# A blocked triangular inverse inside an RWKV-7 layer: joining two passes of small products, and splitting one level into 32x32 blocks

## What is computed

```python
sa = jnp.einsum('bhvk,bhk->bhv', S, kk_t)
S = (S * w_t[:, :, None, :]
     - sa[..., None] * (kk_t * a_t)[:, :, None, :]
     + v_t[..., None] * k_t[:, :, None, :])
y = jnp.einsum('bhvk,bhk->bhv', S, r_t)
```

## Time and profile before

| what | value |
| --- | --- |
| median of 3 runs | 2400.12 us (2399.1 to 2400.26) |
| span of the profiled execution, first to last instruction | 2399.3 us |
| its mean granted PE clock | 0.998 |
| PE busy | 2361.7 us, 98% |
| DVE busy | 1534.4 us, 64% |
| ACT busy | 1209.0 us, 50% |

### The profile page before, as it was taken

How to read it: one execution, slowest core, us unless ns; L and a number is a source line. 1 busy time by engine, 2 the same in 40 slices (tenths; PEclk the granted TensorE clock), 3 DMA queues, 4 the chain that set the end, 5 groups by cost and what they waited for, 6 DMA issues and landing times.

```text
span 2399.3 us, 49369 instructions
## 1 busy us (share of the span) xinstructions
PE 2361.7 (98%) x20503; PEld 2229.2 (93%) x20503; DVE 1534.4 (64%) x1893; ACT 1209.0 (50%) x1590; POOL 17.1 (1%) x36
## 2 busy tenths in 40 slices
PE   9999999989999999999999999999999999999998
PEld 9999799879998899999999999999999888999886
DVE  8588588566774455657799875656745444555445
ACT  5586563354464466755644346465544333444343
POOL 0000000000000000000000000000000000000000
PEclk9999999999999999999999999999999999999999
DMA  9355566325556644564566565655666666666664
GB/s 285 116 184 175 178 191 187 99 74 179 180 169 187 189 151 158 180 201 141 158 193 179 165 184 167 185 179 150 199 199 173 191 190 186 185 184 183 193 186 148
DMA packets 216554, 419.90 MB, mean 175 GB/s; under 512 B 17056, under 2 KB 19440, under 8 KB 215648
## 3 DMA queue, kind: packets, MB, share of 16 engines
q1 hardware_dynamic: 207520, 397.98, 54.5%
q0 software_dynamic: 2560, 10.59, 1.4%
q10 hardware_dynamic: 6288, 8.61, 1.3%
HBM read 410.84 MB, written 6.29 MB: 174 GB/s over the span
## 4 chain that ended last, share of the span: by engine, by line
PE 92%; DVE 5%; ACT 2%; issue 1%; DMA 0%; DVEq 0%; ACTq 0%
PE ps L504 28%; PE ps L505 28%; PE ps L506 28%; DVE wlo L369 1%; PE ps L724 1%; ACT whi L365 1%; PE ps L652 1%; PE ps L638 1%; PE ps L732 0%; PE ps L988 0%; DVE regions L1978 0%; PE ps L869 0%; DVE act_lo L2292 0%; PE ps L749 0%; PE ps L1003 0%
## 5 line engine op out<-in xcount | busy, mean ns | idle before, releaser
L369 DVE TENSOR_TENSOR wlo<-wraw,whi 128x1024 fp32r<-128x1024 f32 x752 | 916.4, 1223 | 786.9 <-ACT whi L365 785.6
L365 ACT ACTIVATE whi<-wraw 128x1024 fp32r<-128x1024 f32 x752 | 793.4, 1058 | 1040.3 <-PE ps L506 1021.7
L504 PE MATMUL ps<-act_hi,whi 128*128 128x256 f32 (+2 forms) x4480 | 1274.8, 285 | 10.5 <-DVE act_lo L2292 7.4
L505 PE MATMUL ps<-act_lo,whi 128*128 128x256 f32 (+2 forms) x4480 | 1261.2, 282 | 0.0
L506 PE MATMUL ps<-act_hi,wlo 128*128 128x256 f32 (+2 forms) x4480 | 1259.8, 281 | 0.0
L504 PEld LDWEIGHTS ps<-act_hi,whi 128*128 128x128 f32 x4480 | 842.7, 188 | 17.9 <-issue 12.6
L505 PEld LDWEIGHTS ps<-act_lo,whi 128*128 128x128 f32 x4480 | 845.4, 189 | 1.1
L506 PEld LDWEIGHTS ps<-act_hi,wlo 128*128 128x128 f32 x4480 | 843.0, 188 | 0.0
L505 PE MATMUL ps<-wlo,regions_r 128*128 128x512 f32 x512 | 202.2, 395 | 0.0
L504 PE MATMUL ps<-whi,regions_r 128*128 128x512 f32 x512 | 202.2, 395 | 0.0
L506 PE MATMUL ps<-whi,regions_r 128*128 128x512 f32 x512 | 202.2, 395 | 0.0
(11 more groups left out here) (369 smaller groups left out, 1477.6 us busy)
## 6 DMA issues: line engine op xcount, KB each, us to landing
wraw<-in_a_w_in SPq DMA_DIRECT2D x128, 512.0 KB, 3.8
wraw<-in_w_up SPq DMA_DIRECT2D x128, 512.0 KB, 3.8
wraw<-in_w_down SPq DMA_DIRECT2D x128, 512.0 KB, 3.7
wraw<-in_w_in SPq DMA_DIRECT2D x112, 512.0 KB, 3.8
wraw<-in_b_w_qg SPq DMA_DIRECT2D x64, 512.0 KB, 4.0
wraw<-in_a_w_out SPq DMA_DIRECT2D x32, 512.0 KB, 4.1
wraw<-in_w_k_shared SPq DMA_DIRECT2D x32, 512.0 KB, 3.8
wraw<-in_w_v_shared SPq DMA_DIRECT2D x32, 512.0 KB, 4.2
```

The costliest lines, as they stand in the source:

```text
L365: nc.scalar.activation(whi[:, q % RING], wraw[:, q % RING], ACT.Copy).then_inc(hi_ready, 1)
L369: nc.vector.tensor_tensor(wlo[:, q % RING], wraw[:, q % RING], whi[:, q % RING].bitcast(F32), ALU.subtract).then_inc(lo_ready, 1)
L504: mm(o, hi_s, hi_m, start=first, stop=False, skip_group_check=True)
L505: mm(o, hi_s, lo_m, start=False, stop=False, skip_group_check=True)
```

## The change

The two passes of "ab" become one step, in which f alternates product by product. The PE wait of the step for the bank's earlier content (c > 1) is for both halves at once. Level 4 multiplies only the two 32x32 blocks on the diagonal of each 64x64 matrix (`inside_halves`), which doubles the number of products and makes each smaller. Its z products leave the rest of banks 6 and 7 unwritten, so DVE clears both banks once, after the first two transposes, and the first z steps wait for that (`levels_clear`) in place of `blocks_ready`. The z products of level 5 move to banks 4 and 5, so that 6 and 7 stay clear.

```diff
-            steps_at[AB_AT[c]] = [("ab", c, 0, 0), ("ab", c, 1, 0)]
+            steps_at[AB_AT[c]] = [("ab", c, 0, 0)]
...
+            def inside_halves(f, o_bank, lhs, rhs):
+
+                for i, p in SLOTS:
+                    for h in range(2):
+                        at, c_ = half_rows(p, h), half_cols(8 * f + i, h)
+                        m_ = mm(ps[at, o_bank, half_cols(i, h)], lhs[at, c_], rhs[at, c_], start=True, stop=True)
+                return m_
...
                 if kind == "ab":
                     if c > 1:
-                        pe.wait_ge(S["ab_ready"], 2 * c - 3 + f)
+                        pe.wait_ge(S["ab_ready"], 2 * c - 2)
...
-                    into_tokens((f,), AB_BANK[c], key(Bc, c), chan(KR, 0, ts), sig=S["ab_mm"], over=1)
+                    into_tokens((0, 1), AB_BANK[c], key(Bc, c), chan(KR, 0, ts), sig=S["ab_mm"], over=1)
...
-                    m_ = within_tokens(f, 4 + f, flat(AB[c % 2]), flat(Tm)) if lv == 4 else across_halves(f, 4 + f, AB[c % 2], Tm, 1)
+                    m_ = inside_halves(f, 4 + f, AB[c % 2], Tm) if lv == 4 else across_halves(f, 4 + f, AB[c % 2], Tm, 1)
...
-                        pe.wait_ge(S["blocks_ready"], 5)
+                        pe.wait_ge(S["levels_clear"], 1)
...
-                    m_ = within_tokens(f, 6 + f, flat(Yl), flat(TTs[:, c])) if lv == 4 else across_halves(f, 6 + f, Yl, TTs[:, c], 0)
+                    m_ = inside_halves(f, 6 + f, Yl, TTs[:, c]) if lv == 4 else across_halves(f, 4 + f, Yl, TTs[:, c], 0)
...
-                        st.do(stt(late_cols, heads(bank(6 + f), 8)[:, :, 32:64], cs("causal")[:, 32:33], late_cols, ALU.mult, ALU.add), sig["lv_t"])
+                        st.do(stt(late_cols, heads(bank(4 + f), 8)[:, :, 32:64], cs("causal")[:, 32:33], late_cols, ALU.mult, ALU.add), sig["lv_t"])
...
                     if (s, u) == (2, 1):
                         for f in range(2):
                             first_turn(0, f)
+                        st.do(nc.vector.memset(bank(6, 2), 0.0), sig["levels_clear"])
```

More of the change, by code:

```diff
@@ L160, in program @@
             act_step dve_step gi_ready ss_done sq_ready rn_ready rnr_ready rnx_bc bcm_ready rk_ready rk_bc rk_taken gain_loaded
-            bonus_ready bonus_first gsq_ready late_loaded0 late_loaded1 silu_ready gate_stored ab_mm ab_ready ab_stored ab_loaded ab_packed inv_ready inv_ones v_centred ks_fixed blocks_mm blocks_ready am_mm am_ready first_mm state_mm tok_mm tok_ready lv_y lv_ysb lv_z
+            bonus_ready bonus_first gsq_ready late_loaded0 late_loaded1 silu_ready gate_stored ab_mm ab_ready ab_stored ab_loaded ab_packed inv_ready inv_ones v_centred ks_fixed blocks_mm blocks_ready levels_clear am_mm am_ready first_mm state_mm tok_mm tok_ready lv_y lv_ysb lv_z
             lv_m lv_t gn_var gn_std warm_ready w_mm w_sb u_mm u_sb y_mm y_sb m_mm m_sb yn_ready zt_mm z_f
```

## The result

The changed kernel takes 2407.17 us (median of 7 runs, 2403.19 to 2410.91) against 2400.12 (7 runs, 2399.1 to 2401.29): 1.0031 [1.0022, 1.004], slower by 7.05 us by the medians (the ratio and its interval come from all runs, so they need not be those of the medians). The forecast was 2397.3 and the range ended at 2402.5.

What follows compares the result with a forecast made beforehand. PE, busy 98% of the span, was taken as the bound. The terms 0 - 6.3 + 2.3 + 0.6 + 0.3 + 0.3 gave -2.8 us, so 2400.12 - 2.8 = 2397.3 us, range 2394.0 to 2402.5.

Steps and rivals of the forecast that it cites:

- "ab": Steps ahead of the gather: 3.0 us saved on PE becomes waiting for DVE's packing; counted 0, bounds 0 and -3.0.
- The price of a step: Level 4: a new step costs what a level 5 step does, 0.79 us less; eight steps save 6.3 us.
- four tiles are no better than two: Slower rival, level 4: tiles writing one bank exclude each other, 0.2 us dearer a step; 2402.0 us, chance 0.12.
- The waits: Levels 4 and 5: PE then waits on DVE's transposes and clearing; 0.6, 0.3 and 0.3 us in the sum.
- wait (2): 4y of chunk 3: its second call comes at 437.8 and waits 0.3 us for DVE's transpose.
- Wait (1): Second 5y call: 0.31 us late for DVE's second transpose; counted in two chunks, 0.6 us.
- The portions: Levels' dense places: PE uses up fetched instructions before the next portion, 1.0 to 1.5 us late each; 2.3 us counted.
- half of the places be hit: Of one dense place in each of four chunks, two are late by 1.15 us: 2.3 us, bounds 0 and 6.
- Portions take longer beside the weights: Slower rival, levels: at 4.84 us a portion, 17.3 us a chunk, +6.4 us; 2406.5 us, chance 0.07.
- a fetch took no longer there: Argument against longer portions in the levels: a fetch takes 1.1 us each there, 1.2 in the scan.
- Idle PE put down to nothing, at distances of one portion: Sign in the levels: some 2 us of unexplained idle PE, at distances of 128 records, confirms late instruction portions.
- a scan of the same length: Sign in the scan: four whole added portions leave its boundaries, so it moves as a whole and lasts as long.

Runs made afterwards that it cites:

- "ab" alone: The kernel before with only the joined "ab" step, level 4 as before; 2400.86 us, 1.0003.
- gather_warm: The changed kernel with 14 dummy products, results unread, ahead of the gather's wait for the packing; 2404.38 us, 1.0023 against the kernel before.
- half_blocks: gather_later with only the first of level 4's two 32x32 blocks computed, the other left out; 2398.01 us, 0.9987 against the kernel before.
- load_later: gather_later with POOL's load of chunk 3 held until both 4z calls of chunk 2 are done; 2402.56 us, 1.0005 against the kernel before.
- no_load: gather_later without POOL's load of chunk 3, which then works on other products; 2402.32 us, 1.001 against the kernel before.
- gather_later: The changed kernel with the gather two half slabs later (12 in place of 10); 2408.91 us, 1.003 against the kernel before.
- level4_alone: The changed kernel with "ab" in two passes again, so only level 4 changed; 2406.64 us, 1.0029 against the kernel before.

## Why the prediction was wrong, and where it was right

- **"ab": right in its rows, wrong in its bound.** The step took 1.16 us as forecast, and the gather waited 3.27 for DVE where I had said about 3.5. What failed is "None of it reaches the end. [...] I count 0; the bounds are 0 and -3.0": there was no bound on the side of a loss. After the wait of 3.27 us PE ran on at 0.50 of its clock, which cost 2.55 us behind the gather in the profiled execution; in the medians of "ab" alone it is 0.6, not told from zero, and between after and gather_warm 2.9, with intervals that overlap. This is the smaller of two failures.
- **The price of a step: right.** 128 records on four tiles in turn took 1.35 us against 2.08, so 0.73 is saved where I had taken 0.79, and the rival "four tiles are no better than two" fell: it needed some 2.2. The Trainium skill (TensorEngine Tiling (Array Packing), Gotcha 1: PSUM Pressure) has different row tiles shut out of one bank at the same time; here four of them wrote one bank at 1.35 / 128, about 11 ns a record, and the trace does not agree.
- **The waits: right, but for one that did not come.** The clearing took 0.91 us where I had taken 0.9. The first 4z came 3.37 us after 4y; the forecast was 392.45 - 389.32 = 3.13, and 0.22 is the stop inside 4y. The second 4y call of chunk 3, wait (2), stood for 0.24 us at 448.38; I had said 0.3. Wait (1), 0.6 in the sum, is not seen: the 5y steps of after are unbroken.
- **The portions: the step that failed, a term that was mis-sized.** The mechanism was there, but I let "half of the places be hit: 2 x 1.15 = 2.3 us, bounds 0 and 4 x 1.5 = 6". PE stopped at a whole portion seven times, for 0.22, 0.71, 0.35, 0.86, 4.49, 1.08 and 0.86 us, 8.6 in all, and by the estimate above about 4.5 more went with the clock behind the longest: some 13 us where 2.3 stood and 6 was the bound. Level 4, forecast at about -2.8 with its waits, cost 6.4 alone. The 3.74 us a portion that I used came from the scan, where DMA engines have little to do (0.02). From 393.74 to 397.51, 3.77 us, it holds; from 424.57 to 433.37, beside the load, it was 8.80. The 1.0 to 1.5 us a place were too little even at the quiet pace: I took the densest 128 records to need 2.7 us, but the 4z step alone has 128 in 1.35, and gather_warm stood 2.52 us in a portion of 3.86. And no term allowed for the clock behind a stop.
- **The rival I put away.** "Portions take longer beside the weights" gave 2406.5 and I gave it 0.07. That 2407.17 came out so near is luck: it had every chunk at 17.3 us, and the chunks took 15.60, 14.80, 24.70 and 18.31, with the loss in one portion and the clock behind it. I put it away since "a fetch took no longer there", 1.1 against 1.2 us. That row times the packets while they move. The delay lies ahead of them: the packet moved six microseconds after the portion began, where 1.2 to 1.9 were usual, and then took about 1.3 us (an estimate: 5.0% of 16 engines over 1.6 us). A busy share cannot show a wait in a queue. The Trainium skill (Runtime: NRT & Kernel Launch, Instruction fetch mechanics) calls crossing such a boundary mostly hidden; in this stage it was not.
- **What came out as listed.** Idle PE put down to nothing, at distances of one portion, and a scan of the same length: 74.30 against 74.99 us. The added instructions were four portions, as counted: the queue of fetches has 149 packets over the span where it had 145.

**Shown:** the loss is level 4's (parts alone), goes with the number of instructions (half_blocks), and its worst stop follows POOL's load (load_later); the stops are waits for a fetch (the packet ahead of each); the gather's part is clock (rows of gather_warm). **Argued only:** that the spread of after's runs, 2403 to 2411, is that of a fetch whose lateness differs from one execution to the next. **Open:** why a packet waits while other transfers pass, and in what order they go. Moving the load moved the stop, yet without the load 2.36 us stayed beside a slab of weights; the queue of fetches shows when its packets move, not when they were asked for. Open too is how long a stop must be before the clock falls: it fell behind 2.09 us in load_later and not behind 2.36 in no_load.

## What to carry to other kernels

Cutting a product into more, smaller ones on more tiles can be cheaper on PE and still lose, for it is paid in instructions: count the records in a portion, compare the densest portion (not the mean) with the time of a fetch, and price that fetch by the DMA traffic of the stage that is changed, not by a quiet one. Then ask what the clock does behind the longest stop. A saving ahead of a wait with a fixed end turns into idle time and can cost clock behind it; move the waiting step back (here 1.6 to 2.0 us were got by that), or look at the granted clock before counting such a saving at zero. How long a transfer took tells nothing of how long it waited to begin.

## What the runs showed of the hardware

- PE stops after whole portions of 128 products' records (with their loads 256 instructions). From one portion's begin to the next it took 3.40 and 3.77 us in after where PE had to wait; 5.39 (load_later) and 5.66 (no_load) as a slab of weights passed; 7.44 (gather_later), 7.70 (level4_alone) and 8.80 (after) beside a slab and POOL's load, two transfers of 256 KB.
- Before each of 27 stops at whole portions, in eleven traces (all seven of after, two of the scan of before, the longest of nine other runs), one packet of the fetch queue moved 2.1 to 3.0 us ahead of the moment at which PE resumed.
- The clock fell to 0.50 after waits of 3.27 and 4.49 us, and to 0.60 from 344 to 348, where one of 3.28 ended at 344.34; the same wait filled with products (28 in 3.29 us) kept 1.00. It also fell to 0.50 behind a stop of 2.09 (load_later) and stayed at 1.00 behind one of 2.36 (no_load).
- Four 32x32 tiles in turn into one bank took 128 records in 1.35 us, where two took 64 in 1.20.
